# The second half of each weight slot is loaded from GpSimd's queue instead of SyncE's

## The reference

```python
z = rms_norm(h) @ w_in + b_in                      # 1024 x 5120
h = h + (sigmoid(ga) * (attention(q, k, v) @ w_pa) + sigmoid(gc) * (short_conv(u) @ w_pc)) @ w_o
...
def expert_block(args):                            # 32 experts, 2 per token
    xb, e = args
    hdn = jax.nn.silu(xb @ w1[e]) * (xb @ w3[e])   # w1, w3: 1024 x 512
    return hdn @ w2[e]                             # w2: 512 x 1024
...
h = h + gate * (p @ w_ple_proj)
# second block
h = h + concat(gla, nsa) @ w_out
h = h + cross_attn(h, mem)                         # xa_wq, xa_wk, xa_wv, xa_wo
h = h + peer_ffn(h)                                # tables down, up: 16384 x 1024 each
```

## Time and profile before

| | before |
|---|---|
| runs | 1941.63, 1944.14, 1944.42 us |
| median | 1944.14 us |
| profiled execution, its own time | 1941.77 us |
| its span | 1940.0 us |
| PE busy | 1712.7 us, 88% of the span |
| DVE, ACT, POOL busy | 896.2, 718.6, 5.5 us |
| DMA queue q1 (SyncE's) | 398.59 MB, 55.0% of 16 engines' span |
| DMA queue q10 (ScalarE's) | 17.87 MB, 2.7% |
| mean granted clock of PE | 0.938 of full speed |

### The profile page before, as it was taken

How to read it: one execution, slowest core, us unless ns; L and a number is a source line. 1 busy time by engine, 2 the same in 40 slices (tenths; PEclk the granted TensorE clock), 3 DMA queues, 4 the chain that set the end, 5 groups by cost and what they waited for, 6 DMA issues and landing times. The chain is left out here.

```text
span 1940.0 us, 26483 instructions
## 1 busy us (share of the span) xinstructions
PE 1712.7 (88%) x10833; PEld 1344.6 (69%) x10833; DVE 896.2 (46%) x1528; ACT 718.6 (37%) x1436; POOL 5.5 (0%) x25
## 2 busy tenths in 40 slices
PE   6999986667766767998998899989999999999997
PEld 5988553223322334688658599989999988888886
DVE  3563320000000002235634349998788976666665
ACT  3453121001001001343333244434777755554454
POOL 1000000000000000000000000000000000000000
PEclk9999998788878888997799999999999999999999
DMA  9434469999999997433011115545444445555553
GB/s 346 167 139 145 173 248 421 421 422 421 421 421 421 422 421 283 168 136 109 1 44 44 66 55 185 185 152 178 160 131 131 133 160 192 192 194 194 195 194 132
DMA packets 84948, 418.18 MB, mean 216 GB/s; under 512 B 14091, under 2 KB 16592, under 8 KB 51930
## 3 DMA queue, kind: packets, MB, share of 16 engines
q1 hardware_dynamic: 73440, 398.59, 55.0%
q10 hardware_dynamic: 11386, 17.87, 2.7%
HBM read 415.36 MB, written 1.06 MB: 215 GB/s over the span
## 5 line engine op out<-in xcount | busy, mean ns | idle before, releaser
L2436 DVE TENSOR_TENSOR tab_lo<-arena,tab_hi 128x1024 fp32r<-128x1024 f32 x256 | 312.3, 1224 | 121.3 <-ACT tab_hi L1885 119.2
L1057 PE MATMUL bank<-arena 128*32 128x512 f32 x1536 | 230.3, 754 | 145.0 <-DMA arena<-in_w_dram 143.4
L1885 ACT CAST tab_hi<-arena 128x1024 fp32r<-128x1024 f32 x256 | 267.9, 1047 | 0.2
L1057 PEld LDWEIGHTS bank<-arena 128*32 128x32 f32 x1536 | 63.1, 134 | 284.6 <-issue 282.6
L1469 PE MATMUL bank<-x_hi,tab_lo 128*128 128x256 f32 x1024 | 144.2, 284 | 7.9 <-DVE tab_lo L2436 7.9
L1469 PE MATMUL bank<-x_hi,tab_hi 128*128 128x256 f32 x1024 | 148.3, 288 | 2.0 <-ACT tab_hi L1885 2.0
L2118 DVE TENSOR_TENSOR arena<-arena,bank 128x512 f32<-128x512 f32 x8 | 5.5, 688 | 298.9 <-PE bank L1075 298.9
L1469 PE MATMUL bank<-nT_lo,tab_hi 128*128 128x256 f32 x1024 | 141.8, 280 | 0.0
L1502 PE MATMUL bank<-tab_hi,e_hi 128*128 128x512 f32 x512 | 136.9, 389 | 1.8 <-DVE arena L2475 1.8
L1469 PEld LDWEIGHTS bank<-x_hi,tab_lo 128*128 128x128 f32 x1024 | 131.7, 191 | 8.3 <-DVE tab_lo L2436 8.3
L1502 PE MATMUL bank<-tab_hi,e_lo 128*128 128x512 f32 x512 | 136.8, 389 | 0.0
(11 more groups left out here) (395 smaller groups left out, 2330.1 us busy)
## 6 DMA issues: line engine op xcount, KB each, us to landing
arena<-in_w_dram SPq DMA_DIRECT2D x192, 1024.0 KB, 21.0
arena<-in_peer_down_dram SPq DMA_DIRECT2D x128, 512.0 KB, 3.7
arena<-in_peer_up_dram SPq DMA_DIRECT2D x128, 512.0 KB, 4.3
arena<-in_packed_first_dram SPq DMA_DIRECT2D x28, 1024.0 KB, 7.6
arena<-in_packed_later_dram SPq DMA_DIRECT2D x28, 1024.0 KB, 7.3
arena<-in_mem_w_dram ACTq DMA_DIRECT2D x8, 1024.0 KB, 9.8
arena<-in_packed_later_dram SPq DMA_DIRECT2D x2, 816.0 KB, 15.3
arena<-in_packed_later_dram SPq DMA_DIRECT2D x2, 768.0 KB, 18.9
```

The lines of the kernel that those rows point to most:

```text
L1057: mm = nc.tensor.matmul(dst[SLOTS * e:SLOTS * e + SLOTS, :], lhsT=lhsT, rhs=moe_weights(step, e)[:, k, :], start=k == 0 and step in (0, 2, ...
L1885: nc.scalar.copy(tab_hi[n % HI][:, :], tab[n % PR]).then_inc(S("table_hi"), 1)
L2436: nc.vector.tensor_tensor(tab_lo[n % PR][:, :], tab[n % PR], tab_hi[n % HI][:, :].bitcast(F32), ALU.subtract).then_inc(S("table_lo"), 1)
```

## The change

A function `load_half(eng, x)` issues the loads of one half of every slot, in the old order and with the old waits. SyncE calls it for x = 0; GpSimd calls it for x = 1, behind its constants. Inside a step of the experts each queue issues two loads (`e in range(x, BATCH, 2)`). Before the first tile of the tables, SyncE now also waits for half 0 of the last six slots.

```diff
+        def load_half(eng, x):
+
+            def load(n, src):
+                width = src.shape[1] // 2
+                if n >= RING:
+                    m = n - RING
+                    if m in spent_at:
+                        eng.wait_ge(S("tile_done"), spent_at[m])
+                    else:
+                        eng.wait_ge(S("moe_steps"), (2 * (m - MOE_AT) + x) // BATCH + 1)
+                cols = slice(width * x, width * x + width)
+                eng.dma_start(slot[n % RING][:, cols], src[:, cols]).then_inc(landed[n % RING][x], 16)
+
+            eng.wait_ge(S("x_in"), 16)
+            for n, pieces in enumerate(first):
+                load(n, w["packed_first"][n][:, 0:filled(pieces)])
+            for b in range(BATCHES):
+                for step in range(STEPS):
+                    src = w[("w1", "w3", "w2")[step // 2]]
+                    for e in range(x, BATCH, 2):
+                        n, half = moe_unit(b, step, e)
+                        assert half == x
+                        if n - RING in spent_at:
+                            eng.wait_ge(S("tile_done"), spent_at[n - RING])
+                        else:
+                            eng.wait_ge(S("moe_steps"), STEPS * b + step - 2)
+                        cols = slice(2048 * (step % 2), 2048 * (step % 2) + 2048)
+                        eng.dma_start(moe_weights(step, e).rearrange("p k n -> p (k n)"),
+                                      src[BATCH * b + e][:, cols]).then_inc(landed[n % RING][x], 16)
+            for m in range(len(later)):
+                load(LATE_AT + m, w["packed_later"][m][:, 0:filled(later[m])])
+
         @block.gpsimd
         def _(pool):
...
             pool.drain().then_inc(S("consts"), 1)
+            load_half(pool, 1)
 
         @block.sync
         def _(sp):
 
-            def load(n, src):
...
-            for m in range(len(later)):
-                load(LATE_AT + m, w["packed_later"][m][:, 0:filled(later[m])])
+            load_half(sp, 0)
 
             dn = w["peer_down_2"]
             upt = w["peer_up_2"][0].rearrange("(i p) d -> i p d", p=P)
             sp.wait_ge(S("tile_done"), tile_no["xo", 1, 1] + 1)
+            for n in range(LATE_AT + len(later) - RING, LATE_AT + len(later)):
+                half_ready(sp, n, 0)
             for n in range(TILES):
```

More of the change, by code:

```diff
@@ L2520, in _, with filled @@
                                                in1=gfin, op0=ALU.mult, op1=ALU.mult).then_inc(S("fin_out"), 1)
+        def filled(pieces):
+            return sum(k * (c1 - c0) for _, k, c0, c1 in pieces)
+        def load_half(eng, x):
[27 more added lines that the diff above has]
+                load(LATE_AT + m, w["packed_later"][m][:, 0:filled(later[m])])
         @block.gpsimd
```

## The result

The changed kernel takes 1952.11 us (median of 5 runs, 1949.33 to 1955.01) against 1944.39 us for the kernel before in the same session (5 runs). The ratio is 1.0041, 95% interval 1.0029 to 1.0053: slower by 0.41%, about 8 us. The forecast was 1945.1 us and no change; 1952.11 lies inside the range of 1937 to 1957, but beyond the likeliest case's own 1949, and the change is clear of the 0.2% that the forecast took for no change. The profiled execution took 1952.33 us, its span is 1950.6 us, against 1941.77 and 1940.0 before.

A forecast was written before the change was run, and what follows sets the result against it. Expert stage bound by DMA at 421 GB/s, elsewhere mostly TensorE. All terms were 0 except +1.0 us for the first slot, added to the 1944.14 us median: 1945.1 us, 8-in-10 range 1937 to 1957 us.

The forecast's parts named there:

- likeliest case: Whole kernel: median 1945.1 us, no change beyond 0.2%, with its own range of 1941 to 1949 us.
- slower: Whole kernel: the outcome of running slower by more than about 0.2% (3.9 us); chance 0.34.
- A: Rival, expert stage: GpSimd's queue costs more per packet, rate falls to 416 GB/s, +6 and +1, 1951 us; chance 0.20.
- The rate of the expert stage: Expert stage: two queues move bytes no faster or slower than one's 421 GB/s and share roughly packet by packet; 0 us.
- C: Rival, expert stage: the second queue fills small packets' cost, 429 GB/s, -9.6 and +1, 1935.5 us; chance 0.15.
- B: Rival, first slot: unfair sharing puts one half behind up to six of the other queue, +11.5 us, 1956 us; chance 0.08.
- Issue time: SyncE and GpSimd queues: 55 us of issuing leaves SyncE, worth 0; GpSimd's 127 issues of 0.33 to 2.44 us cost 0.
- The first slot: Slot 0, ScalarE's copy of line 769: GpSimd's half lands later, copy at 13.6 to 15.6; 0 to +1.7, taken as +1.0 us.
- Order inside a step: Expert steps: four halves in two parallel pairs finish when all four have been moved, as before; 0 us.
- ScalarE's loads: Biases and `mem_w` loads meeting two queues: slower landings (`mem_w` grows by 2.5 us), but nobody waits; 0 us.
- SyncE's new wait: Before the first table tile at 1103.0: ring loads are issued by 1020.1, 83 us earlier, so the wait costs 0.
- TensorE's wait for `in_w_dram`: Sign in the expert stage: the wait stays at 143 us within 5 if the forecast is right.

The follow-up runs named there:

- experts_halves: Against the kernel before, GpSimd issues only half 1 of the expert slots (96 loads), SyncE all others; 1946.89 us, ratio 1.0018.
- give_back: Against the kernel before, GpSimd issues half 1 of the first 84 expert slots, SyncE all else including the last 12; 1943.75 us, ratio 0.9998.
- dense_halves: Against the kernel before, GpSimd issues half 1 of the 31 dense slots, SyncE all expert loads; 1954.90 us, ratio 1.0061.
- experts_steps: Against the kernel before, GpSimd issues all four halves of every second expert step (96 loads), SyncE the rest; 1949.94 us, ratio 1.0043.
- slot_0_pieces: Against the kernel before, GpSimd issues only half 1 of slot 0, cut into four loads of 32 rows; 1953.84 us, ratio 1.0052.
- slot_0_leads: Against the kernel before, GpSimd issues only half 1 of slot 0, and SyncE's first load waits for GpSimd's signal; 1951.47 us, ratio 1.0040.

## Why the prediction was right or wrong

**The number: inside the range, and partly by luck.** The forecast was +1.0 us and the measured change is +7.7, 0.41%, past the 3.9 us that the forecast set as the line for no change; of its own cases, "slower" (0.34) came. 1952.11 is in the range because the upper end, 1957, was set by twice the price of A, and A's mechanism is not what happened.

**The rate of the expert stage: right.** 421 GB/s and equal shares. A and C are refuted by these rows. B, which expected equal shares in steady work too, is not; it was priced at the first slot, 7 x 2.49 us, with the copy after 20. The copy at 17.99 refutes that price, but a small form of B's mechanism is what happened there: 1.50 MB of the other queue went ahead, not 6.3.

**Issue time: right.** GpSimd's issues take 0.53 us in the median, inside the bounds of 0.33 to 2.44, and hid in its idle time.

**The first slot: the right mechanism, mis-sized.** The step was "with SyncE's lag of 1.0 us its first bytes come at 7.7; with two us more [...] at 9.7". They came at about 11.7. The rest of the working holds: 11.7 + 4.98 + 0.9 = 17.6, and 17.99 was measured. The term is +4.1, not +1.0. Of the 4.0 us by which 11.7 is later than 7.7, 0.7 are GpSimd's issue at 7.39 instead of 6.70, and 3.3 the lag of 4.3 instead of 1.0. The bound was taken from how long an issue may take (this one took 0.7), and the cause was elsewhere: half of slot 0 went behind up to 1.5 MB of the other queue. The sentence "from there it has half the engines, since SyncE's queue holds six halves" had that queue in view, but only as one that shares.

**Order inside a step: wrong.** The term stood at 0 and measured 2.6 us. "The last of the four lands when the four have been moved, either way" holds only if nothing else is moved meanwhile. In the ring's three steps there is always something else: halves that SyncE may already load. A queue that starts 1 MB ahead and then shares evenly stays ahead, and the reader waits for the other: 2.6 us here, 3.1 in `experts_halves`, given back in `give_back`. At the exit the same holds for the `later` slots. There the change itself loses little, because the half of them on each queue stands behind that queue's own experts: 0.15 us from mid-stage to the last step, against 8.1 in `dense_halves`.

**ScalarE's loads: right.** `mem_w` lands after 11.7 us instead of 9.8 (12.3 was reckoned), the biases after 28.0 and 34.1 us (28.6), and nobody waits.

**SyncE's new wait: right.** The waits of SyncE's queue in 950:1130 (us in total, times, longest):

```profile
SPq L2613 <- PE bank L717: 78.4, 1, 78.4
SPq L446 <- DMA arena<-in_packed_later_dram: 4.7, 1, 4.7
```

4.7 us once. Together with the 78.4 us for TensorE that is 83.1; the kernel before waited 82.9 us for TensorE at this place.

Of what should show it, TensorE's wait for `in_w_dram` stayed in its band (142.0 us), and that told nothing: lateness at a stage's entry shifts the waits and leaves their sum. The start of the copy at 17.99, between the bands of the forecast and of B, told it.

**What stays open.** From the start of the last step to the end of the span the changed kernel loses 2.3 us more, and other kernels -0.7 to 2.5; `give_back` is level at the last step and 2.3 us late at the end of its span, but only 0.8 in the median. The traces say where: 1.2 of the 2.3 us are in the last step itself (6.08 us for 4.91, granted clock 0.59 for 0.73), and the rest in the next 25 us (clock 0.86 in 746.24:770 for 0.93 in 736.77:760); from there on the distance stays as it is. `give_back` shows the same (6.19 us, 0.58 and 0.86). `dense_halves`, with 0.72 and 0.93, loses nothing there. The 1.6 us at 253 us came in five profiled executions (the changed one, `dense_halves`, `experts_steps`, `slot_0_pieces`, `slot_0_leads`: 3.58 to 3.88 us for the 18 matmuls, at a granted clock of 0.50) and not in the others (2.25 us). So both go with TensorE's clock; what decides it was not tried, nor how much of it is in the medians. Whether SyncE would lag behind a GpSimd load in front was not tried either. No version ran faster than before.

## What to carry to other kernels

One queue is also an order: it delivers bytes as the reader needs them, and splitting a stream over two queues gives up that order even when the rate is untouched. Before splitting, look for the places where one queue is ahead of the other (starts, restarts, the hand-over to the next stage), count the bytes that can pass ahead of needed ones, and divide by the rate: 3.41 MB at 421 GB/s were 8.1 us. If a second queue must be used, leave the last stretch before a hand-over to the queue that leads (24 MB gave the whole lead back here).

## What the hardware showed that was not expected

- A load of GpSimd issued just behind one of SyncE's moved nothing until SyncE had moved about one load (0.96 and 1.01 MB), or 1.50 and 1.64 MB where SyncE had issued several; then both moved 27 packets each in the us that was read. Alone it started 1.2 to 1.4 us after its issue.
- GpSimd's queue alone moves 421 GB/s with rows of 8 KB, and half of 421 beside SyncE's, to within two packets (12270 and 12272).
- Four loads to 32 partitions each, beside full ones, pulled the total from 400 to 235 GB/s.
- A drain on GpSimd behind a load ended only when the load had landed (SyncE issued at 13.11, the load's last bytes moved shortly before 13).
